# The squares of the residual norm: a tree of adds on GpSimd and two products with ones per block

## What is computed

```
def rms_norm(x, w):
    y = x * rsqrt(mean(x * x, axis=-1) + 1e-6)
    return y * w

mix = mamba2_mixer(rms_norm(h, a_norm_pre), ...)          # layer 0
h = h + rms_norm(mix, a_norm_post)
ffn = conv_ffn(rms_norm(h, f_norm_pre[0]), ...)
h = h + rms_norm(ffn, f_norm_post[0])
kv = rms_norm(h, kv_norm) @ w_kv                          # layer 1
mix = attention(rms_norm(h, b_norm_pre), kv, ...)
h = h + rms_norm(mix, b_norm_post)
ffn = conv_ffn(rms_norm(h, f_norm_pre[1]), ...)
h = h + rms_norm(ffn, f_norm_post[1])
```

## Time and profile before

| | us |
|---|---|
| median of 3 runs | 2727.0 (2725.07 to 2728.11) |
| profiled execution | 2726.28 |
| its span | 2724.5 |
| TensorE busy | 2657.2 (98%) |
| VectorE busy | 1478.4 (54%) |
| ScalarE busy | 950.5 (35%) |
| GpSimd busy | 609.6 (22%) |

### The profile page before, as it was taken

The page is one execution under the profiler, slowest core; times in us unless marked ns, Lnnn a source line. Parts: engine busy times, 40 slices in busy tenths (PEclk is TensorE's granted clock), DMA queues, the critical chain, the costliest instruction groups (busy, mean ns, idle before and its releaser), DMA issues.

```text
span 2724.5 us, 44585 instructions
## 1 busy us (share of the span) xinstructions
PE 2657.2 (98%) x18246; PEld 1804.7 (66%) x18246; DVE 1478.4 (54%) x1898; ACT 950.5 (35%) x1742; POOL 609.6 (22%) x410
## 2 busy tenths in 40 slices
PE   8899999999999999999999998999999999999998
PEld 5566666666656666666666665688666666666665
DVE  6576767777587754545401276675176445453113
ACT  4333333344233433232211255576253332322121
POOL 1042544443233100010122111121421000101121
PEclk9899999999999999999999998998999999999999
DMA  3111111010031111111111001100101111111111
GB/s 109 39 34 37 32 39 40 31 33 32 32 126 38 32 54 46 54 46 54 61 43 64 26 32 47 32 2 2 47 32 48 53 46 54 46 57 54 53 53 62
DMA packets 38042, 123.97 MB, mean 46 GB/s; under 512 B 3360, under 2 KB 12704, under 8 KB 37920
## 3 DMA queue, kind: packets, MB, share of 16 engines
q1 hardware_dynamic: 37920, 122.25, 13.7%
HBM read 118.04 MB, written 4.19 MB: 45 GB/s over the span
## 4 chain that ended last, share of the span: by engine, by line
PE 90%; DVE 5%; ACT 2%; issue 2%; POOLq 0%; DVEq 0%; POOL 0%; ACTq 0%; DMA 0%
PE PS L1807 25%; PE PS L1809 25%; PE PS L1808 25%; PE PS L2024 2%; PE PS L1893 2%; PE PS L2216 2%; PE PS L2230 1%; PE PS L2232 1%; PE PS L2031 1%; PE PS L2054 1%; PE PS L2016 1%; DVE UB L1300 1%; PE PS L2249 1%; PE PS L2042 1%; PE PS L2250 1%
## 5 line engine op out<-in xcount | busy, mean ns | idle before, releaser
L1807 PE MATMUL PS<-R,whi 128*128 128x384 f16 (+1 forms) x3168 | 987.4, 312 | 14.1 <-DVE wlo L1266 11.3
L1808 PE MATMUL PS<-R,whi 128*128 128x384 f16 (+1 forms) x3168 | 987.1, 312 | 0.0
L1809 PE MATMUL PS<-R,wlo 128*128 128x384 f16 (+1 forms) x3168 | 986.9, 312 | 0.0
L1266 DVE SCALAR_TENSOR_TENSOR wlo<-stage,whi 128x1024 f16<-128x1024 f32 (+1 forms) x182 | 246.1, 1354 | 733.0 <-ACT whi L699 732.9
L1807 PE MATMUL PS<-BIG,whi 128*128 128x384 f16 (+1 forms) x1452 | 452.3, 312 | 12.2 <-issue 8.3
L1809 PE MATMUL PS<-BIG,wlo 128*128 128x384 f16 (+1 forms) x1452 | 452.2, 311 | 0.0
L1808 PE MATMUL PS<-BIG,whi 128*128 128x384 f16 (+1 forms) x1452 | 452.2, 311 | 0.0
L1807 PEld LDWEIGHTS PS<-R,whi 128*128 128x128 f16 x3168 | 311.3, 98 | 178.9 <-issue 13.1
L1808 PEld LDWEIGHTS PS<-R,whi 128*128 128x128 f16 x3168 | 311.2, 98 | 162.6 <-issue 9.2
L1809 PEld LDWEIGHTS PS<-R,wlo 128*128 128x128 f16 x3168 | 311.3, 98 | 157.4 <-issue 1.0
L643 POOL TENSOR_TENSOR BIG<-TT,BIG 128x1040 f32 x44 | 96.7, 2198 | 799.8 <-ACT BIG L1121 799.8
(11 more groups left out here) (240 smaller groups left out, 3260.0 us busy)
## 6 DMA issues: line engine op xcount, KB each, us to landing
stage<-wa SPq DMA_DIRECT2D x164, 512.0 KB, 3.4
stage<-wd SPq DMA_DIRECT2D x32, 704.0 KB, 4.0
hT<-h SPq DMA_DIRECT2D x4, 1536.0 KB, 11.3
out<-hT SPq DMA_DIRECT2D x4, 768.0 KB, 3.5
hT<-h SPq DMA_DIRECT2D x2, 1088.0 KB, 10.0
out<-hT SPq DMA_DIRECT2D x2, 512.0 KB, 2.8
pr<-prm SPq DMA_DIRECT2D x1, 328.0 KB, 6.5
BIG<-wdt SPq DMA_DIRECT2D x1, 128.0 KB, 10.4
```

What stands on the lines that cost most here:

```text
L1266: eng.scalar_tensor_tensor(out=WL[d][:, 0:width], in0=stage[:, slot, 0:width], scalar=WS, in1=WH[d][:, 0:width], op0=ALU.mult, op1=ALU.sub ...
L1807: eng.matmul(acc, WH[slot][:, ws], x(0, k, b), start=first, stop=False)
L1808: eng.matmul(acc, WH[slot][:, ws], x(1, k, b), start=False, stop=False)
L1809: return eng.matmul(acc, WL[slot][:, ws], x(0, k, b), start=False, stop=last)
```

## The change

For the norms behind p = 0, 1 and 2 (`q > 0` in `mean_pre`), GpSimd adds the eight squares of a block in place, in two trees of four: tiles 0+1, 2+3 and their sum, then 4+5, 6+7 and their sum; each half-sum is signalled by the new semaphore `h_sq_sum`. TensorE takes one product with ones for each half-sum. The first norm (`q == 0`) keeps its eight products. `h_sq_used` counts one for each block there, so that ScalarE's wait in `pre` has another number.

```diff
+            def residual_squares(q_, b):
+                i = 24 * q_ + 8 * ORD.index(b)
+                for half in range(2):
+                    k0 = 4 * half
+                    for k in (k0, k0 + 2):
+                        eng.wait_ge(h_sq, i + k + 2)
+                        eng.tensor_tensor(sq_slot(q_, k, b), sq_slot(q_, k, b), sq_slot(q_, k + 1, b), ALU.add)
+                    eng.drain()
+                    eng.tensor_tensor(sq_slot(q_, k0, b), sq_slot(q_, k0, b), sq_slot(q_, k0 + 2, b),
+                                      ALU.add).then_inc(h_sq_sum, 1)
+
             def boundary(p, q, j0, mix):
                 tail_squares = post_squares(p, j0, mix)
                 tail_squares(ORD[0])
+                if q is not None:
+                    residual_squares(p + 1, ORD[0])
                 tail_squares(ORD[1])
                 if q is not None:
                     lows(q, ORD[0])
+                    residual_squares(p + 1, ORD[1])
                 tail_squares(ORD[2])
                 if q is not None:
                     lows(q, ORD[1])
+                    residual_squares(p + 1, ORD[2])
                     lows(q, ORD[2])
...
             def pre(q, b):
-                eng.wait_ge(h_sq_used, 24 * q + 8 * block_rank(q, b) + 8)
+                eng.wait_ge(h_sq_used, 8 * (b + 1) if q == 0 else 24 + 3 * (q - 1) + ORD.index(b) + 1)
...
+                if q > 0:
+                    for half in range(2):
+                        eng.wait_ge(h_sq_sum, 6 * (q - 1) + 2 * ORD.index(b) + half + 1)
+                        r = eng.matmul(PS[:, bank, 0:n], onesD[:, :], sq_slot(q, 4 * half, b), start=(half == 0),
+                                       stop=(half == 1))
+                    r.then_inc(h_sq_used, 1)
+                    return
```

More of the change, by code:

```diff
@@ L288, in program @@
         h_sq, h_sq_used, pre_rsqrt = sem("h_sq"), sem("h_sq_used"), sem("pre_rsqrt")
+        h_sq_sum = sem("h_sq_sum")
         x_normed, xn_hi, xn_lo_v = sem("x_normed"), sem("xn_hi"), sem("xn_lo_v")
@@ L1889, in mean_pre @@
                     eng.wait_ge(pre_rsqrt, 3 * q + ORD.index(b))
+                if q > 0:
[5 more added lines that the diff above has]
+                    return
                 for k in range(KD):
-                    i = 24 * q + 8 * block_rank(q, b) + k
-                    eng.wait_ge(h_sq, i + 1)
+                    eng.wait_ge(h_sq, 8 * b + k + 1)
                     eng.matmul(PS[:, bank, 0:n], onesD[:, :], sq_slot(q, k, b), start=(k == 0),
```

## The result

The changed kernel takes **2762.5 us** (median of 4, 2761.2 to 2764.2) where the kernel before took 2727.6 (2725.1 to 2729.1) on the same chip: a ratio of 1.0129, 95% interval 1.0112 to 1.0147. The forecast was 2761.0, with a range of 2741 to 2779. The profiled execution after has a span of 2759.6 us, 35.1 over the 2724.5 of before.

The account below looks back on a forecast made before the run. TensorE, with 90% of the chain that ended last, was taken to bound the kernel. 2727.0 plus 13.8, 2.2 and 13.5 us at the three boundaries and 4.4 of clock gave 2761 us, range 2741 to 2779.

Parts of the forecast that it names:

- The sum: Added time: 13.8 us at the first boundary, 13.5 third, 2.2 second, 4.4 for TensorE's clock, 33.9 in all.
- the clock's halves: First and third boundary: slower TensorE clock after 4.5 us waits ahead of block 0's second product, 2.2 us each.
- B: From TensorE's first output-mean product at the first boundary to that at the second: 13.8 us plus 2.2 of clock.
- E: From TensorE's first output-mean product at the third boundary to the end: 13.5 us plus 2.2 of clock.
- C: Second boundary, from TensorE's first output-mean product to the query projection's first product: 2.2 us late.
- A: From the start to TensorE's first output-mean product at the first boundary; the prediction added no time there.
- What is removed and added: Three boundaries: 54 TensorE products fewer, 31.5 us if nothing waits; 54 GpSimd adds of 1.0 or 0.77 us more.
- GpSimd's order: Boundaries: tail squares queue behind the trees; block 0's tail tiles end 12.0 us late at the first.
- the walk: Step-by-step timing through the boundaries from trace durations: 13.8, 2.2 and 13.5 us late at first, second and third.
- VectorE: Residual updates at the boundaries: GpSimd's adds hold each by 0.67 us for 384 columns, 0.48 for 272.
- The first rival: Boundaries: adds don't slow VectorE, only GpSimd's queue order and the clock are left: 2736 us; 0.12 with its neighbours.
- The second rival: Half-sums cost next to nothing and the clock stays up, gain at the second boundary: -7.5 us, 2719.5; chance 0.04.

Follow-up runs that it names:

- The idle writes: Kernel before, TensorE keeping eight products; GpSimd writes zeros at the places of the additions, with nobody waiting for them: 2740.5 us.
- writes: Changed kernel with GpSimd's additions replaced by writes of zeros of about the same length, same waits, sums left out: 2734.1 us.
- Keeping TensorE busy there: Kernel with trees and two products at the second boundary alone (2729.2 us), plus 60 small float16 products ahead of one wait there: 2728.7 us.
- the idle additions: Kernel before, TensorE keeping eight products; GpSimd makes the additions in the same places into a stretch nobody reads: 2760.5 us.
- the float16 products: Kernel before, no trees, float16 squares and ones for the three later norms, or for the first norm too: 2717.7 and 2715.9 us.
- the first kernel: Kernel before, no trees, float16 squares and ones for the three later norms alone: 2717.7 us.
- 32 products ahead of the waits: Changed kernel plus 32 small float16 products on TensorE ahead of its waits for a block's second half-sum, all but one: 2762.6 us.

## Why the prediction was right, and where it was mis-sized

**The sum.** It had 13.8 + 13.5 + 2.2 + 4.4 = 33.9 us; the medians differ by 34.9, the spans by 35.1. With the clock's halves put to their boundaries, B was forecast at 16.0 and measured +16.0, E at 15.7 and +15.7. C was 2.4 us over its forecast, and in the trace A, which the change doesn't touch, was 1.2 shorter: that the span came within 1.2 us of the sum is in part luck.

**What is removed and added.** The time taken from TensorE showed as forecast: two products and a wait where eight stood. The additions of 384 columns took 1.21 us on average beside VectorE (1.16 at the third boundary; 1.0 was assumed), 1.08 behind the drain. The last square of block 1 ended at 845.00 and its half-sum let TensorE go 2.7 us later, the upper value assumed. That was at 847.72 in place of 848.6 forecast; with the 1.2 us by which this execution was ahead at the first mark, this is 0.3 late. By groups of lines and shapes:

```profile
L636 POOL TENSOR_TENSOR R<-R 128x384 f32<-128x384 f32 x16 | 19.4, 1211 | 61.3 <-ACT R L752 61.3
...
L638 POOL TENSOR_TENSOR R<-R 128x384 f32<-128x384 f32 x8 | 8.6, 1080 | 1.1
```

**GpSimd's order.** The three tail tiles of block 2 stood without gaps behind the tree, and ScalarE's square of block 0's output began 57.4 us behind the mark (887.97 - 830.58) in place of 44.9 (876.70 - 831.77): 12.5 late, 12.0 forecast. The idle writes show this step almost alone, at 7.2 and 7.6 us with its clock (the walk had 5.3 and 5.7, with 2.2 of clock each 7.5 and 7.9).

**VectorE.** Three or four updates a block stretched from 0.61 to 1.35 us, 0.74 each where 0.67 was assumed. The first rival (no slowing, 2736) was measured almost as itself: 2734.1 with writes. This one step decided 28 of the 35 us, less what the shorter writes give.

**The second boundary and the clock: the terms that were mis-sized.** C was forecast at 2.2 and came at 4.6. The prediction gave the clock 2.2 us each at the first and third boundary and nothing at the second, since it looked for waits of 4.5 us ahead of block 0's second product and held that in the middle of a boundary a slower clock is hidden by the next wait. At the first and third that holds. Behind the mean of output 0 the clock fell, and block 0's first product came 17.32 us behind the third head tile's start (908.07 - 890.75) in place of 15.60; this shortened the wait ahead of the second product to 2.70 us (2.36 at the third boundary), and the half-sum, not TensorE, still set the time. The clock fell behind these shorter waits too, so the 2.2 us came out near (1.7 and 1.8) with a wait that was mis-sized. But a wait doesn't decide it by its length: block 1's at the third boundary, 2.90 us, left the clock at 1.00. TensorE in the 4 us behind the mean of output 0, behind block 0's second product, and behind that wait:

```profile
890.75:894.75 4.00, 4.00 (x15) 0.56 0.65 182
911.39:915.39 4.00, 4.00 (x14) 0.58 0.02 4
2005.40:2009.40 4.00, 4.00 (x31) 1.00 0.02 4
```

At the second boundary the slower clock isn't hidden: TensorE's tiles there are long and full, the wait of 3.85 us stands ahead of them, the mean of output 2 comes later and with it the chain of VectorE and ScalarE that sets the end. Keeping TensorE busy there gave back 2.6 us. At the first and third boundary the same means gave back 1.7 and 1.8.

**What else is shown.** The new wait for the half-sums is a small part of the loss. The totals with nobody waiting and with the change are close (2760.5 and 2762.5), but the trace of the idle additions has 2.8 us in D that the changed kernel's has not; at the boundaries the difference is 4.8 us. Beside writes, where VectorE isn't held, two products in place of eight are worth 2.1 us in B, 5.4 in C and 1.9 in E. Beside additions they are worth -1.7, -1.9 and -1.1: TensorE, ahead of time, waits for a sum that ends up to 2.7 us behind the last square, and its clock falls behind the wait. With the clock kept up the boundaries cost +14.4, +2.8 and +14.0, where the idle additions cost +14.3, +2.7 and +14.6, so the two products then neither gain nor lose in B and C. The time saved on the busiest engine turned into waits there. The second rival (faster, if additions cost almost nothing) put the worth of free half-sums at 7.5 us; the float16 products, where no sum stands behind the last square, gave 8.9 at the boundaries in the first kernel, and 8.8 and 9.7 of the whole.

## What to carry to other kernels

Before work goes from a full engine to an idle one, look at who reads SBUF beside it: GpSimd's additions held VectorE's two-operand updates, and these stood ahead of everything that the saved TensorE time was to bring forward. In an engine's written order, a step that waits for late data holds every ready step behind it, so it goes behind them or is split. Where products with ones are the cost, a cheaper product (float16 here) takes the time away without a new dependence; and behind a new wait (from 2.4 to 3.9 us here, though not behind each) the clock of TensorE is a term of the sum wherever full tiles follow, not only at the end of a stage.

## What the runs showed of the hardware that was not expected

**The attention moves by itself.** Stretch D has the same instructions in all kernels and took 325.5 to 331.4 us; A, which hardly differs in all but the last, took 830.4 to 833.5. In D most of the difference lies in one dip of the granted clock, which stands at the same work in the kernels looked at and has another length; some of it lies in the first 30 us of D, with a clock of 0.87 before and 0.84 to 0.92 in the others. The 30 us from 240 to 270 us behind the query projection's first product, in the kernel before, with the idle additions, and with 32 products ahead of the waits (columns as above):

```profile
1882.05:1912.05 30.00, 29.02 (x202) 0.72 0.01 1
```

```profile
1899.68:1929.68 30.00, 29.02 (x187) 0.62 0.01 1
```

```profile
1900.10:1930.10 30.00, 29.02 (x191) 0.64 0.00 1
```

TensorE was busy 29.02 us of 30 in all three, the granted clock 0.72, 0.62 and 0.64 on average. Why the same work gets a longer dip is not shown, nor whether it changes from one execution of a kernel to the next, since there is one trace of each. It means that a comparison of two traces by their span carries some 3 us from stretches that the change doesn't touch. The stretches around the change agreed better, but not always to tenths: C differs by 1.7 us between the two float16 kernels, which are the same there.

**Half a filler worked at one wait and not at another.** Ahead of block 1's second product, 1.95 us of small products left a wait of 1.55 us at the first boundary and one of 2.08 us at the second. The granted clock of the 4 us behind was 1.00 at the first and 0.67 at the second. So a clock that falls is to be looked for in the rows behind each wait, and not judged by the wait's length.
